# Three more row slots for two weight slots and an output buffer in a streaming encoder with a PEER layer

## The reference, cut to what matters

```
h  = rmsnorm(x) * (1 + scale1) + shift1          # shift, scale, gate from silu(c) @ w_ada
z  = h @ w_in                                    # 18 column blocks of 128
x += gate1 * (concat(pool(zA), gmlp(zU, zV), diff_attn(zQ, zK, zVV)) @ w_out)
h2 = rmsnorm(x) * (1 + scale2) + shift2
q  = h2 @ w_pq                                   # 8 heads x 2 halves x 128
...                                              # top 16 of 128 keys per half, top 16 of the pairs: 128 experts a token
a  = sum_d u_tab[e, d] * h2[d]                   # 128 rows of 1024 floats a token
w  = softmax(score) * gelu(a)
x += gate2 * sum_e w[e] * v_tab[e]               # 128 more rows a token
```

## Time and profile before

| | |
|---|---|
| median of three runs | 2499.09 us |
| the profiled execution, its own time | 2497.03 us |
| its span, first to last instruction | 2495.1 us |
| busy: PE / DVE / ACT / POOL | 1285.8 / 1373.1 / 284.0 / 1490.4 us |
| moved by DMA | 969.15 MB, mean 388 GB/s |
| of that by POOL's queue / by SP's | 850.53 / 117.22 MB |
| mean granted TensorE clock | 0.723 |

### The profile page before, as it was taken

How to read it: one execution, slowest core, us unless ns; L and a number is a source line. 1 busy time by engine, 2 the same in 40 slices (tenths; PEclk the granted TensorE clock), 3 DMA queues, 4 the chain that set the end, 5 groups by cost and what they waited for, 6 DMA issues and landing times.

```text
span 2495.1 us, 21880 instructions
## 1 busy us (share of the span) xinstructions
PE 1285.8 (52%) x7582; PEld 710.9 (28%) x7582; DVE 1373.1 (55%) x3238; ACT 284.0 (11%) x616; POOL 1490.4 (60%) x1601
## 2 busy tenths in 40 slices
PE   4987766586400255454665376688430023333554
PEld 2646655452000132222321066565100000000111
DVE  1316998745499945445341478846369974444000
ACT  1223312210000110100100042221000000000000
POOL 2111545565777656566667665545777677777774
PEclk7988877797555587677888687799765555556788
DMA  9997998999999999999999999899999999999998
GB/s 372 390 408 261 348 409 316 407 409 381 408 409 409 351 394 409 376 391 409 409 409 409 407 408 409 313 382 341 397 410 409 385 410 409 409 409 407 407 409 332
DMA packets 267749, 969.15 MB, mean 388 GB/s; under 512 B 38036, under 2 KB 38548, under 8 KB 261240
## 3 DMA queue, kind: packets, MB, share of 16 engines
q0 software_dynamic: 227968, 850.53, 86.5%
q1 hardware_dynamic: 39664, 117.22, 12.5%
q10 hardware_dynamic: 8, 0.01, 0.0%
HBM read 962.38 MB, written 5.27 MB: 388 GB/s over the span
## 4 chain that ended last, share of the span: by engine, by line
DMA 30%; DVE 26%; PE 22%; POOL 11%; issue 6%; ACT 2%; SPq 2%; POOLq 0%; DVEq 0%; ACTq 0%
DVE ring L765 18%; DMA ring<-in_v,eV 16%; DMA ring<-in_u,eU 13%; POOL ring L434 8%; PE ps L1222 7%; PE ps L1433 5%; POOL ring L429 3%; PE ps L1265 3%; PE ps L1405 2%; DMA wada<-in_wada 1%; PE ps L1123 1%; SPq L347 1%; PE ps L1239 1%; ACT L446 1%; SPq L373 1%
## 5 line engine op out<-in xcount | busy, mean ns | idle before, releaser
L765 DVE CUSTOM_DVE_ANT_0 ring<-ring,ps 128x1024 f32<-128x1024 f32 x768 | 904.1, 1218 | 486.5 <-DMA ring<-in_u,eU 358.2
L429 POOL DMA_INDIRECT ring<-in_u,eU x768 | 729.0, 949 | 497.5 <-issue 165.4
L434 POOL DMA_INDIRECT ring<-in_v,eV x768 | 728.7, 949 | 345.4 <-issue 174.3
L1222 PE MATMUL ps<-ring,Wd 128*32 128x512 f32 x3072 | 555.6, 861 | 646.8 <-DMA ring<-in_v,eV 643.6
L1222 PEld LDWEIGHTS ps<-ring,Wd 128*32 128x32 f32 x3072 | 114.4, 138 | 1009.4 <-issue 1004.6
L1433 PE MATMUL ps<-h,wring 128*128 128x128 f32 (+1 forms) x1024 | 193.8, 346 | 19.3 <-ACT h L523 14.8
L1433 PEld LDWEIGHTS ps<-h,wring 128*128 128x128 f32 x1024 | 164.5, 203 | 77.3 <-issue 58.0
L1265 PE MATMUL ps<-h,wring 128*128 128x128 f32 (+1 forms) x768 | 145.4, 353 | 26.9 <-DVE h L829 15.3
L1265 PEld LDWEIGHTS ps<-h,wring 128*128 128x128 f32 x768 | 129.3, 211 | 48.9 <-issue 35.5
L974 DVE MAX8 sv<-sc 128x8 f32<-128x128 f32 x160 | 40.6, 287 | 184.9 <-ACT sc L441 183.1
L1198 PE MATMUL ps<-cst,eF 128*128 128x128 f32 x6 | 2.7, 451 | 239.9 <-DVE eU L1086 239.9
(11 more groups left out here) (204 smaller groups left out, 1089.8 us busy)
## 6 DMA issues: line engine op xcount, KB each, us to landing
wada<-in_wada POOLq DMA_DIRECT2D x42, 1024.0 KB, 15.5
wring<-in_win SPq DMA_DIRECT2D x72, 512.0 KB, 7.2
wring<-in_wpq SPq DMA_DIRECT2D x64, 576.0 KB, 7.5
wring<-in_wout SPq DMA_DIRECT2D x32, 512.0 KB, 7.3
ring<-in_u,eU POOLq DMA_INDIRECT x768, 8.1
ring<-in_v,eV POOLq DMA_INDIRECT x768, 9.3
wada<-in_wada SPq DMA_DIRECT2D x6, 1024.0 KB, 9.8
wring<-in_ckT SPq DMA_DIRECT2D x8, 512.0 KB, 6.7
```

What stands on the lines that cost most here:

```text
L429: g.indirect_dma_start(ring[p % NR][:], None, a["u"], bass.IndirectOffsetOnAxis(ap=eU[t % 3][:, i:i + 1], axis=0)).then_inc(ld_r[p % NR], 16)
L434: g.indirect_dma_start(ring[p % NR][:], None, a["v"], bass.IndirectOffsetOnAxis(ap=eV[t % 3][:, tok:tok + 1], axis=0)).then_inc(ld_r[p % N ...
L765: nc.vector.tensor_tensor_reduce(ring[p % NR][:], ring[p % NR][:], ps[:, 0:2, :].rearrange("p b d -> p (b d)"), 1.0, 0.0, ALU.mult, ALU.ad ...
L1222: ins = mm(ps[QUAD * q:QUAD * q + QUAD, 2 + half, :], Wd[:, QUAD * q + c, :], ring[at4[q] % NR][:, half * 512:(half + 1) * 512], start=(c ...
```

## The change

`ring` gets 18 slots in place of 15, `wring` 4 in place of 6, and the buffer `ysb` is given up. Tile t's output now goes through the first 1024 floats of a partition of `hg[0]` (t = 0, 3, 4, 5) or `hg[1]` (t = 1, 2). ACT's copy waits, beside what it waited for, for the last `tokens` that read that buffer. `mpart` moves into the room of `ring`'s slot 6. In bytes of a partition: +12288, -9216 and -4096.

```
-NWR = 6
+NWR = 4
...
-NR = 15
+NR = 18
...
-        YS = room(D * 4)
-        ysb = at("ysb", [D], YS)
...
-        mpart = [at(f"mpart{s}", [512], YS + s * 2048) for s in range(2)]
+        mpart = [at(f"mpart{s}", [512], G0 + 6 * 4096 + s * 2048) for s in range(2)]
...
+        ysb = [hg[int(t in (1, 2))][:].rearrange("p k n -> p (k n)")[:, 0:D] for t in range(TILES)]
...
                 act.wait_ge(v_pe, NBATCH * (t + 1))
                 if t:
                     act.wait_ge(y_add, t)
-                copy(ysb[:], ps[:, 2:4, :].rearrange("p b d -> p (b d)")).then_inc(y_ev, 1)
+                act.wait_ge(htok_pe, (1, 3, 3, 4, 4, 4)[t])
+                copy(ysb[t], ps[:, 2:4, :].rearrange("p b d -> p (b d)")).then_inc(y_ev, 1)
...
-                y = ysb[:].rearrange("p (k b s) -> p k b s", k=KD, b=NB)
+                y = ysb[t].rearrange("p (k b s) -> p k b s", k=KD, b=NB)
...
-                step(tt(x[:].rearrange("p k n -> p (k n)"), x[:].rearrange("p k n -> p (k n)"), ysb[:], ALU.add), y_add)
+                step(tt(x[:].rearrange("p k n -> p (k n)"), x[:].rearrange("p k n -> p (k n)"), ysb[t], ALU.add), y_add)
...
-                    ins = nc.tensor.transpose(ps[:, 2 + k // 4, k % 4 * P:(k % 4 + 1) * P], ysb[:, k * P:(k + 1) * P], idn)
+                    ins = nc.tensor.transpose(ps[:, 2 + k // 4, k % 4 * P:(k % 4 + 1) * P], ysb[t][:, k * P:(k + 1) * P], idn)
```

## The result

The changed kernel takes 2481.6 us (median of five runs, 2479.15 to 2483.49) against 2498.52 us for the kernel before beside it (five runs, 2494.66 to 2500.82). The ratio is 0.9931, 95% interval 0.9921 to 0.9942: 16.9 us faster, where the prediction had 20.1 us (2499.09 to 2479). In the profiled executions the span went from 2495.1 to 2479.4 us, 15.7 us less, and the mean granted clock from 0.723 to 0.737.

A forecast was written before the change was run, and what follows sets the result against it. Bound: DMA at 409 GB/s, with short stalls where the row ring is full and unused. Profiled time 2497.03 - 26.8 (row slots) + 7.65 (unit 0 losses) = 2477.9 us, 2479.9 against the median, stated as 2479; range 2467 to 2494 us.

The forecast's parts named there:

- More row slots: Three more row slots save 3.85 us in each of six stall cycles and 3.7 in the seventh: 26.8 us less.
- SP's order: Unit 0: SP's outputs and x wait behind out chunk 7's load, 5.95 us later, all on the path; bounds 3, 6.
- pq: Unit 0: with four weight slots pq loads come late, mostly hidden behind DVE: 1.2 us more; bounds 0 and 16.
- POOL's pause: Sign in the profile: POOL pauses after the eighteenth gather, about 3.7 us shorter than 15.3.
- Nothing in later units, nothing for the output through h: After unit 0 fewer weight slots cost nothing; the output through h and moving `mpart` add no wait: 0.
- PE waiting for `wring` outside unit 0: Sign that would show the prediction wrong: PE waits for weight loads in a unit other than unit 0.
- Every stall pays: Rival: each of the nine stall windows pays, 34.5 us gained, 2470 to 2472 us; chance 13%.
- POOL is too slow: Rival: POOL cannot fill 18 slots, only cycles beside weight loads pay, 15.4 us gained, 2489 to 2491 us; 15%.
- The weight ring starves in unit 0: Rival: loads keep their landing times with fewer in line, start loses 38 us, 2508 us; decides from 27 us; 12%.
- The 0.5 us for z and out: Unit 0: z and out chunks come more slowly with four weight slots: 0.5 us more, 16 us at worst.
- The two sides cancel: Rival: stalls are covered but consumers then run into the same full DMA; within 5 us of before; chance 5%.
- The sum by 358 GB/s a core: Estimate from the Trainium skill's HBM limit: three entries take 4.4 us, so the gain is 30 us; prediction used 409 GB/s.

The follow-up runs named there:

- s17w5: The changed kernel with 17 row slots and 5 weight slots in place of 18 and 4; 2481.77 us, ratio 0.9947.
- s18w4_mid: The changed kernel with unit 0's scores of a pq chunk put into the middle of the next chunk's matmuls; 2477.97 us, ratio 0.9921.
- h_only: The changed kernel with 15 row slots and 6 weight slots as before, keeping the output through h and the moved `mpart`; 2496.72 us, ratio 1.0.
- w4_only: The kernel before with only the weight ring cut, 4 slots in place of 6; 2506.46 us, ratio 1.0044.
- before_moved: The kernel before, 15 and 6 slots, with only unit 0's `out_pool` issued later, after the fourth z load of unit 1; 2489.75 us, ratio 0.997.

## Why the prediction was right

**The bound and the place of the gain: right.** Mean rate 391 GB/s as forecast, calm stretches at 409 as before, and the gain where DVE's and PE's fronts leave the ring full.

**More row slots, -26.8 us: right in kind, some 3 us too large.** Measured 23.8 us in the profiled executions and 23 to 25 over the four kernels with 18 slots. The step that was mis-sized is "six give 3.85 us": the seven gave 3.4 on the mean. By the bytes moved the six from 390 on gave 3.8 each, the first cycle gave 2.0 (the lateness went from 8.1 to 6.1), and 0.8 was lost behind 2100; why at these two places is not shown. Cycles were the right unit: 810 with 860 and 1580 with 1700 paid once each, and nine paying windows would have been 34.5 us. Of the 64 us of the nine windows, 37 were to remain; the same places show some 47 us after, but their bottoms are only the part of a stall that the windows caught, and part of the gain lies ahead of them (370:390). The stair, not those windows, is the measure.

**SP's order, +5.95 us: too large, and inside its own bounds.** The load of out chunk 7 does wait for out chunk 3, but that chunk itself ran at 169.41 and not at 170.81, so `out_pool` moved by 4.5 us. Of this only 1.0 us reached the first pq load in these two traces, since x's issue, behind the small pieces, got shorter by 3.4 us. PE's chunk 0 was 3.4 us late all the same, as from the issue of its load to its start there were 10.9 us in place of 8.4. The means over the nine traces tell it with less chance in it: `out_pool` and x together held SP for 21.1 us with six slots and for 18.0 with four, and 4.0 us of 7.3 reached chunk 0. "The whole 5.95 us go onto the path" is the step that was too large; the lower bound, 3 us "if the small pieces of `out_pool` drain faster later", had the mechanism. The forecast of 197 us for the first pq load was wrong (191.80), the first gather's +7 to 8 us too (the fifteenth came at 262.30, +4.4).

**pq, +1.2 us: too small, and for a wrong reason.** "From there DVE is the bound and PE's lateness is hidden" is the step that failed. The lateness grew from 3.4 us at chunk 0 to 8.1 at chunk 15, 4.7 us in all, and the second half of the indices took all of it, through DVE's wait for `rs` (3.81 us in place of 0.20); s17w5, where nothing grows behind chunk 2, and s18w4_mid, with 2.9 of the 4.7 us taken away, bear this out. The prediction did not have unit 1's norm in DVE's path. With 0.20 us of waiting before, that place had no slack. Taken together the start was forecast at 7.65 us (with 0.5 for z) and measured at 8.1: two errors of opposite sign, a right total by luck. The granted clock adds luck of its own: the sum of squares took 5.38 us in h_only and 3.69 before, with a granted clock of 0.66 in 236:241 and 1.00 in 237:242, and the halves of the indices lie 35.0 and 33.3 us apart.

**POOL's pause: wrong, for the same reason.** It was to shrink by 3.7 us and stayed at 15.24. The deeper ring did take 3 x 1.24 = 3.7 us off its beginning; but its end hangs on the second half, which was 8.1 - 4.4 = 3.7 us later than the first. In s17w5, where both halves are equally late, the pause is 2 x 1.24 us shorter, as that arithmetic says. The four traces whose halves lie 35.0 us apart bear it out too: with 13, 14, 15 and 16 slots they pause 20.28, 19.02, 17.77 and 16.48 us. s17w5:

```profile
276.41 0.94 POOL L430 DMA_INDIRECT ring<-in_u,eU  x1 [12.80 <-DVE adot L767]
```

**Nothing in later units, nothing for the output through h: right in time, but one sign of being wrong came up.** The prediction named "PE waiting for `wring` outside unit 0", and PE does so once, for 15.04 us at unit 1's pq chunk 0, since SP's order was priced for unit 0 alone. It cost nothing: w4_only loses nothing after unit 0. h_only is even. POOL waited for eU once, as before (73.6 us against 67.7, ahead of the first gather). Landings of u entries in calm stretches became longer by 1.1 us (8.7 against 7.6 at 650:690) where up to 3.85 was said; over all u entries the median rose by 3.4.

**The rivals.** "Every stall pays" falls with the stair (23.8, not 34.5). "POOL is too slow" would have left 15.4 us of gain in four cycles; 605 and 1965, which it excluded, paid in full. Half of its mechanism is there, though: in 650:690 of the changed kernel POOL issues 33 gathers one behind the other and is not held up by a full ring, which fits the 1.1 us by which landings grew there, where three more entries in line would have given up to 3.85. "The weight ring starves in unit 0" had its mechanism half right, as the ring does starve, but with a start loss of 8.1 us and not 38; it needed 27. The 0.5 us for z and out cannot be told from scatter: PE waited 4.8 us for z and ck loads ahead of out, which it did not before, and out chunk 3 ran 1.4 us earlier, but over the six traces with six slots it ran at 166.4 to 171.1. "The two sides cancel" is out by the interval. The sum by 358 GB/s a core is out by the rows: the calm stretch runs at 409 and 410 GB/s in the two kernels.

**The sum.** Forecast -26.8 + 7.65 = -19.2 us, measured in the profiled executions -23.8 + 8.1 = -15.7, by medians -16.9. The difference is the size of a cycle's gain. (Among the chances, what is left of the second rival and the last one are 0.03 + 0.05 = 0.08, not 0.07.)

## What to carry to other kernels

A deeper ring in front of a saturated DMA buys its depth in bytes once per cycle from starved to starved, not once per stall; count the cycles, and take somewhat less than the full depth for each (here 3.4 us of 3.85). When the room for it is taken from another ring, price the phase in which the smaller ring works alone, chunk by chunk to its *last* chunk. Before calling lateness hidden, look for everything that stands behind the last chunk in the late engine's order and at whoever waits for it: here it was the next unit's norm, and not the work on the chunk itself. Taking that norm out of the second half's path was not tried. Then repair that phase: here two small edits of unit 0 gave 9 us more.

## What the runs showed of the hardware that was not expected

- An output in small pieces can hold up the queue that issues it beyond its own issue. In the kernel before `out_pool` takes 14.20 us of SP and x's load behind it 7.82; started 4.5 us later they take 13.99 and 4.44, and without the pieces x takes 0.43 (1.19 in before_moved). It is not the pieces alone: the same two outputs take 6.40 us in unit 2 of the kernel before (at 1090.71) and 1.34 at 227.60 in before_moved. Moving the pieces out of the way alone gave 7.2 us, nearly half of what the whole change gave.
- Queue depth has a cliff. From 18 slots down to 15 the calm rate (650:690) stays at 409 or 410 GB/s; at 14, 13 and 12 it is 398, 373 and 336.
- The landing of a gather grows with the number of slots and says nothing of trouble: the medians over all u entries are 8.1 us with 15 slots, 9.5 with 16, 11.1 with 17 and 11.5 with 18, at a rate that is the same or better.
